# Feature rows on all partitions: by transfers through DRAM on GpSimd's queue in place of TensorE and ScalarE

## What is computed

```python
c_act = jax.nn.silu(c)
for i in range(2):
    mod = c_act @ w_mod[i] + b_mod[i]                      # 6 x 1024 features
    sh1, sc1, g1, sh2, sc2, g2 = jnp.split(mod, 6, axis=-1)
    h = modulate(rmsnorm(x, norm_mix[i]), sh1, sc1)
    y = pool_mixer(h, ...) if i == 0 else moba_attention(h, ...)   # pool_mixer ends in * pool_scale
    x = x + g1[:, None, :] * y
    h = modulate(rmsnorm(x, norm_mlp[i]), sh2, sc2)
    x = x + g2[:, None, :] * squared_relu_mlp(h, w_up[i], w_down[i])
return rmsnorm(x, norm_final)
```

## Time and profile before

| | us |
|---|---|
| median of 3 executions | 1222.71 (1221.52 to 1223.18) |
| the profiled execution | 1221.15 |
| its span, first to last instruction | 1219.4 |
| TensorE busy in it | 1149.8 (94%) |
| VectorE / ScalarE / GpSimd busy | 807.2 / 590.8 / 53.2 |

### The profile page before, as it was taken

How to read it: one execution, slowest core, us unless ns; L and a number is a source line. 1 busy time by engine, 2 the same in 40 slices (tenths; PEclk the granted TensorE clock), 3 DMA queues, 4 the chain that set the end, 5 groups by cost and what they waited for, 6 DMA issues and landing times.

```text
span 1219.4 us, 18071 instructions
## 1 busy us (share of the span) xinstructions
PE 1149.8 (94%) x7384; PEld 1010.6 (83%) x7384; DVE 807.2 (66%) x1287; ACT 590.8 (48%) x914; POOL 53.2 (4%) x103
## 2 busy tenths in 40 slices
PE   5899999999999999999999579999989998999997
PEld 5767659999988776999998479999979887999996
DVE  5558257777776666787777759677783656655554
ACT  6344455444455666644344554434365544543442
POOL 1100000000000001000000000000010000000000
PEclk9999999999999999999999689999999998999999
DMA  8423157977758988798775039877635433555530
GB/s 313 164 74 139 35 211 288 353 269 271 300 143 164 163 129 137 309 356 308 269 271 222 15 136 369 306 272 270 255 131 181 164 114 121 208 199 180 188 124 35
DMA packets 36274, 248.58 MB, mean 204 GB/s; under 512 B 4560, under 2 KB 4704, under 8 KB 7520
## 3 DMA queue, kind: packets, MB, share of 16 engines
q1 hardware_dynamic: 26640, 189.73, 41.5%
q0 software_dynamic: 9552, 57.69, 18.2%
HBM read 242.55 MB, written 4.19 MB: 202 GB/s over the span
## 4 chain that ended last, share of the span: by engine, by line
PE 84%; DVE 10%; ACT 4%; issue 1%; DMA 1%; SPq 0%; DVEq 0%; ACTq 0%
PE bank L1227 71%; PE bank L1409 2%; PE bank L1643 2%; DVE wlo L710 1%; PE bank L1434 1%; PE bank L1626 1%; ACT vo L435 1%; DVE x L730 1%; DVE wlo L821 1%; PE bank L1458 1%; PE bank L1457 1%; PE bank L1456 1%; DVE work L728 1%; PE bank L1305 1%; DVE ul L757 1%
## 5 line engine op out<-in xcount | busy, mean ns | idle before, releaser
L710 DVE TENSOR_TENSOR wlo<-raw,whi 128x2048 fp32r<-128x2048 f32 (+2 forms) x143 | 324.5, 2274 | 103.3 <-ACT whi L425 103.3
L1227 PE MATMUL bank<-uh,whi 128*128 128x256 f32 x1272 | 367.3, 289 | 0.0
L1227 PE MATMUL bank<-uh,wlo 128*128 128x256 f32 x1272 | 359.8, 283 | 0.0
L1227 PE MATMUL bank<-ul,whi 128*128 128x256 f32 x1272 | 359.7, 283 | 0.0
L425 ACT ACTIVATE whi<-raw 128x2048 fp32r<-128x2048 f32 (+2 forms) x143 | 270.4, 1895 | 2.6 <-DMA raw<-in_stream 2.6
L1227 PEld LDWEIGHTS bank<-uh,whi 128*128 128x128 f32 x1272 | 243.5, 191 | 8.4 <-issue 5.9
L1227 PEld LDWEIGHTS bank<-ul,whi 128*128 128x128 f32 x1272 | 243.6, 192 | 4.0 <-issue 1.9
L1227 PEld LDWEIGHTS bank<-uh,wlo 128*128 128x128 f32 x1272 | 243.5, 191 | 0.0
L1227 PE MATMUL bank<-whi,hh 128*128 128x512 f32 x544 | 214.0, 393 | 0.0
L1227 PE MATMUL bank<-wlo,hh 128*128 128x512 f32 x544 | 212.4, 390 | 0.0
L1227 PE MATMUL bank<-whi,hl 128*128 128x512 f32 x544 | 211.8, 389 | 0.0
(11 more groups left out here) (212 smaller groups left out, 1188.8 us busy)
## 6 DMA issues: line engine op xcount, KB each, us to landing
raw<-in_stream SPq DMA_DIRECT2D x176, 1024.0 KB, 4.9
qk<-in_w_mod POOLq DMA_DIRECT2D x48, 1024.0 KB, 5.6
bias_rows<-gb POOLq DMA_DIRECT2D x16, 192.0 KB, 9.3
u<-bias_rows POOLq DMA_DIRECT2D x16, 128.0 KB, 2.4
raw<-in_stream SPq DMA_DIRECT2D x2, 696.0 KB, 10.3
x<-in_x SPq DMA_DIRECT2D x2, 512.0 KB, 4.8
vo<-in_fin_g POOLq DMA_DIRECT2D x2, 512.0 KB, 6.7
out_y<-vo SPq DMA_DIRECT2D x2, 512.0 KB, 2.6
```

What stands on the lines that cost most here:

```text
L710: nc.vector.tensor_tensor(wlo[:, c % RING, 0:w], raw[:, raw_index(c) % RING, 0:w], whi[:, c % RING, 0:w].bitcast(fp32), ALU.subtract).then ...
L1227: ins = mm(out, st, mv, start=start and i == 0, stop=stop and i == 2, skip_group_check=True)
```

## The change

The five rows no longer come from TensorE and ScalarE. GpSimd writes the 8 columns of 128 floats to a DRAM tensor of 5 rows, in the order of the features (`row_to`: 1024 single floats, each to its own address), and later reads one row of 4 KB to all 128 partitions (`row_from`: 512 KB written), after a wait for the write. VectorE waits for `row_in` where it waited for `spread_out`. The waits of TensorE on `col_ready`, `mod_ready` and `spread_out` go with the products. The diff, context cut:

```diff
+        rdram = nc.dram_tensor("feature_rows", [5, D], fp32, kind="Internal").ap()
@@ GpSimd
+            def row_to(k, col):
+                with nc.allow_non_contiguous_dma(reason="1024 features, once a row"):
+                    pool.dma_start(rdram[k, :].rearrange("(b p) -> p b", p=128), col).then_inc(row_out[k], 16)
+            def row_from(k, dst):
+                pool.wait_ge(row_out[k], 16)
+                pool.dma_start(dst, rdram[k, :].partition_broadcast(128)).then_inc(row_in[k], 16)
...
             pool.dma_start(qk[0:64, KI, :], qk[64:128, KI, :]).then_inc(ki_in, 16)
+            pool.wait_ge(col_ready, 2)
+            row_to(0, cact[:, :])
+            pool.wait_ge(s_max["e"], 8)
+            row_from(0, cb[:, :])
             pool.wait_ge(bias_sb, 1)
             for m in range(3):
...
                 elif m == 1:
+                    pool.wait_ge(mod_ready, 1)
+                    row_to(1, gpool[:, :])
                     for h in range(16):
                         pool.wait_ge(used, DIFF + h)
...
                 if m == 1:
                     pool.dma_start(fing, a["fin_g"].partition_broadcast(128)).then_inc(in_fin, 16)
+                    row_from(1, gateb)
                 for i in range(16):
                     g = 16 * m + i
+                    if m == 2 and i == 2:
+                        pool.wait_ge(mod_ready, 2)
+                        row_to(2, mod[:, 40:48])
+                    elif m == 2 and i == 4:
+                        pool.wait_ge(x_ready, x_no(6, 1, 1))
+                        row_from(2, gateb)
...
+            pool.wait_ge(mod_ready, 3)
+            row_to(3, mod[:, 64:72])
+            row_to(4, mod[:, 88:96])
+            row_from(3, cb[:, :])
             pool.wait_ge(bias_out, 256)
             pool.wait_ge(ul_ready, ul_no(8, 0))
...
             pool.dma_start(fing, a["fin_g2"].partition_broadcast(128)).then_inc(in_fin, 16)
+            row_from(4, gateb)
@@ ScalarE: spread_copy and its five calls
-                nc.scalar.activation(dst[:, 512 * j:512 * j + 512], bank[b0 + j][:, :], ACT.Copy).then_inc(spread_out, 1)
@@ VectorE, five times
-            dve.wait_ge(spread_out, 4)
+            dve.wait_ge(row_in[1], 16)
@@ TensorE: spread_col, its five calls and their waits
-                if l != 1:
-                    pe.wait_ge(spread_out, (2, 0, 6, 10)[l])
...
-            pe.wait_ge(mod_ready, 1)
-            spread_col(gpool, 2)
-            pe.wait_ge(spread_out, 4)
             for t in range(NT):
                 norm(5, t)
```

More of the change, by code:

```diff
@@ L244, in build @@
         st_done = [sem(f"st_done{j}") for j in range(2)]
-        col_ready, spread, spread_out = sem("col_ready"), sem("spread"), sem("spread_out")
+        col_ready = sem("col_ready")
+        row_out, row_in = [sem(f"row_out{k}") for k in range(5)], [sem(f"row_in{k}") for k in range(5)]
         mod_ready = sem("mod_ready")
@@ L467, in mlp @@
                     nc.scalar.activation(work[:, 2 + t, :], work[:, t, :], ACT.Square).then_inc(tm_sq, 1)
-                    if t == 0 and l != 1:
-                        spread_copy((0, 1, 2, 4)[l], cb if l == 0 else gateb, 6)
                 hi_upto(m0 + 4)
@@ L498, in pair_upper @@
                     .then_inc(oh_ready, 1)
-            def spread_copy(k, dst, b0):
-                act.wait_ge(spread, k + 1)
-                for j in range(2):
-                    nc.scalar.activation(dst[:, 512 * j:512 * j + 512], bank[b0 + j][:, :], ACT.Copy).then_inc(spread_out, 1)
             act.wait_ge(col_ready, 1)
@@ L649, in _ @@
                 deviation(5, (t,))
-            spread_copy(1, gateb, 2)
             act.wait_ge(mod_ready, 1)
@@ L673, in _ @@
                     value_copy(i // 8, 1, 2, MOBA + i - 1, b_v)
-                    if i == 2:
-                        spread_copy(3, cb, 6)
                 if q == 0 and 1 <= i <= 12 and MIXER[i - 1][0] == "f":
@@ L782, in mlp @@
                 if l == 0:
-                    dve.wait_ge(spread_out, 2)
+                    dve.wait_ge(row_in[0], 16)
                 for s in range(2, 16):
@@ L1182, in _ @@
             mlp(2)
-            dve.wait_ge(spread_out, 6)
+            dve.wait_ge(row_in[2], 16)
             add_and_norm(7, gateb)
@@ L1206, in _ @@
                 lo_beside(MOBA, i, q)
-            dve.wait_ge(spread_out, 8)
+            dve.wait_ge(row_in[3], 16)
             add_and_norm(8, cb)
@@ L1210, in _ @@
             mlp(3)
-            dve.wait_ge(spread_out, 10)
+            dve.wait_ge(row_in[4], 16)
             dve.wait_ge(in_fin, 32)
@@ L1307, in norm @@
                         ins.then_inc(turned, 1)
[L1309 to L1314, removed]
             def mlp(l, turns):
@@ L1369, in mlp @@
                 first(0, 1)
-                if l == 0:
-                    pe.wait_ge(col_ready, 2)
-                    spread_col(cact, 6)
-                elif l == 2:
-                    pe.wait_ge(mod_ready, 2)
-                    spread_col(mod[:, 40:48], 6)
-                elif l == 3:
-                    pe.wait_ge(mod_ready, 3)
-                    spread_col(mod[:, 88:96], 6)
                 first(1, 1)
                 up(2)
-                if l != 1:
-                    pe.wait_ge(spread_out, (2, 0, 6, 10)[l])
                 down(0)
@@ L1755, in _ @@
                     both_halves(MOBA, 7)
-                    pe.wait_ge(mod_ready, 3)
-                    spread_col(mod[:, 64:72], 6)
                 elif kind == "v" and j == 1:
```

## The result

| | before | after |
|---|---|---|
| median, us | 1222.95 (1221.52 to 1225.14) | 1232.83 (1232.17 to 1233.32) |
| ratio to before, 95% interval | | 1.0074 [1.0058, 1.0090] |
| profiled execution / its span | 1221.15 / 1219.4 | 1233.32 / 1231.5 |
| granted clock of TensorE, mean | 0.983 | 0.974 |

The account below looks back on a forecast made before the run. TensorE, busy 94% of the span, was taken to bound the kernel. Gains 5.34 + 2.69 + 1.90 = 9.93 us, no stall added, took the median from 1222.71 to 1212.8 us, range 1211.5 to 1218.

Parts of the forecast that it names:

- Rows 0, 2 and 4: Inside mlp(0), mlp(2) and mlp(3): removing TensorE's row products gains 1.78 us each, 5.34 us in all.
- Row 1: Before pooling, at event 5: ScalarE starts its gained copies earlier without the row copies, a gain of 1.90 us.
- Row 3: Start of MoBA: TensorE goes from the last value product to the features without the row, a gain of 2.69 us.
- Rival 4: Row products only filled TensorE waits, so most of the gain isn't there: 1220.2 us or part of it; chance 0.05.
- Step (b): Bias rows in differential attention, held by row 1's wait for mod_ready: cost zero, up to 6 us for the range.
- Rival 2: Stream falls behind beside bias rows, or mlp(1)'s first w_mod blocks land late: stall 1 to 6 us; chance 0.10.
- Step (a): MoBA start: hanks go behind row 3's write, wait and read, yet arrive in time, 1.3 us remaining; no stall.
- L: Landing time of row 3's column write at the MoBA start, taken as 6 us.
- R: Landing of row 3's broadcast, behind which the hanks queue at the MoBA start: 6.7 us median, 9.5 at worst.
- the limit of 14.0: MoBA start: value in us of column-write landing plus broadcast landing at which late hanks begin to stall TensorE.
- rivals 1 to 3: Rival 1: late MoBA hanks, stall 2.0 to 4.8 us, 0.22. Rival 2: late stream, 0.10. Rival 3: slower, 1225.9 us, 0.05.
- slower: Rival 3: MoBA hanks with write plus broadcast landing above 26.3 us; at worst 13.1 us stall, 1225.9 us; chance 0.05.

Follow-up runs that it names:

- e4: Changed kernel with hanks 0 to 7 ahead of column writes 3 and 4, and row 1's write behind the bias rows: 1215.68 us, ratio 0.9932 to before.
- e8: Kernel before with only rows 0, 2 and 4 through memory, row 4's write behind hank 7; rows 1 and 3 as before: 1220.43 us against 1223.63.
- e5: Changed kernel with the column write as 128 runs of 32 B, output in another feature order: 1226.08 us, ratio 1.0021 to before.
- e9: Changed kernel with bias rows paced two chunks later and hanks 0 to 7 first, row 1's write left in place: 1214.96 us, ratio 0.9937 to before.
- e12: Repeat on another chip: changed kernel with hanks 0 to 7 first and row 1's write behind the bias rows: 1214.86 us against 1223.29 before.
- e1: Kernel before with only a wait for mod_ready added on GpSimd's queue ahead of the sixteen bias rows, no row moved: 1237.98 us against 1225.47.
- e6: Changed kernel with bias rows paced, row h waiting for two more chunks than before: 1224.23 us, ratio 1.0009 to before.
- e7: Kernel before with the wait for mod_ready ahead of the fourth bias row, not the first: 1225.35 us, ratio 1.0011 to before.

## Why the prediction was wrong

**The gains were right, nearly to the number.** Rows 0, 2 and 4: forecast 3 x 1.78 = 5.34, measured 1.8, 1.1 and 1.7 to 1.8, sum 4.7 (e4, e8). Row 1: forecast 1.90, measured 222.2 - 220.3 = 1.9. Row 3: forecast 2.69, measured 2.6 (e4, e5, e9, e12). Sum 9.2 of 9.93. Less the 1.5 us of DIFF it is 7.7, near the 8 us of e4 and e12. Rival 4 falls. The figure of row 4 is the weakest, for the clock is in it: the kernel before had 0.59 and 0.56 from 1024 to 1032, e4 0.69 and then 1.00 from 1020 to 1028. Luck with the clock may have helped there. In the profile of the changed kernel itself two show less: mlp(2) gives 0.6, and mlp(3) 0.1, where the granted clock from 1032 to 1048 was 0.79, 0.50, 0.86 and 0.57.

**Step (b) failed: "I take zero, with up to 6 us for the range".** I had the late start of the bias rows, and that three go out together, but looked at them as a later start of the same train of writes ("for this chunk it starts later and so helps"). The earlier trace rows already held a warning: 8.7 us for a row alone and 17.6 at worst say that rows stand behind one another. Three at once make that queue deeper by one or two just where the stream has 1.2 us to spare. The queue also doesn't stay "full to the end of the layer", in either kernel: before, the rows issued from 372 to 402 took 15.6 to 17.6 us and those from 421 on at most 9.3. The harm is done in the first seven rows. Measured: stream loads of 19.0 us in the median and 20.3 at most became 28.6 and 34.5, ScalarE waited 11.7 us, DIFF +8.1, of which 1.5 are those of e8. e1 shows that the wait alone does it, e6 that it is the rows on their way at once and not the delay. Rival 2 had the mechanism, with 1 to 6 us and a chance of 0.10; both too small.

**Step (a) failed: L was taken as 6, "between" the small moves.** Measured 13.3 to the landing, 13.55 until GpSimd went on, 14.1 with the issue of the read to the hanks. The hank's own landing was 7.3 at the first against R = 6.7. With the prediction's formula L + R = 13.55 + 7.3 = 20.9 against the limit of 14.0 gives a stall of 6.9, and TensorE stood 6.87: the mechanism and the limit were right (that they meet so closely is luck), the term L was mis-sized, 13.55 for 6. The small moves carry 64 runs of 1 KB and 256 runs of 256 B; what counted was the number of runs more than the bytes (e5), and none in the trace had 1024. The rule of the Trainium skill that I quoted against the change (DMA: Bandwidth & Descriptors, Rules for kernel authors: a strided last dimension is one descriptor per element) deserved weight in the choice of L. The runs agree with its direction: 9.0 us against 1.7 with the engines quiet. The same page's 2.0 us plus bytes (Anatomy of one DMA) fits the 128 runs with the engines quiet (1.7); it fails for the 1024 (9.0), and beside other loads for both (4.8 to 10.2 for the 128).

**The clock was not in the sum.** TensorE's long stall was followed by stretches near 1.2 GHz in both places (0.84, 0.50, 0.81 of full speed at MoBA from 936 to 948, 0.63 and 0.51 in DIFF from 412 to 420). It added some 1.7 us at MoBA (8.6 lost for 6.87 idle) and a part in DIFF that I didn't separate. As no run changes the clock alone, its share is argued from the rows and not shown by a run. I had priced stalls at their idle time alone in rivals 1 to 3.

**The rivals together.** Rivals 1 and 2 came true at once. I gave them 0.22 and 0.10 and let each end in the range; neither reached its measured size (8.6 and 8.1), and "slower" was tied to hanks beyond 26.3 us alone. Two losses of separate places add, and that case had no chance of its own.

## What to carry to other kernels

When a transfer is put into a queue ahead of paced transfers, look at what its wait bunches: if the pace of issue is near the time that each takes, a queue once formed drains slowly (here it took the first seven of sixteen rows and a stall), and meanwhile the loads of another queue land late; keep the pace when the start is moved. Price a small transfer by its runs and not by its bytes, and put a write-then-read through memory behind whatever is wanted sooner on that queue. Work taken off the busiest engine brought nearly what its pitch in the timeline said; what decided the sign was the order in the queue that took it over.

## What was not expected of the hardware

- 4 KB as 1024 single floats land after 8.3 to 9.0 us with the DMA engines nearly idle and 11.1 to 17.5 beside other loads, over all kernels here; as 128 runs of 32 B (e5) after 1.7, and 4.8 to 10.2. By the quiet pair, 9.0 and 1.7, 896 more runs cost 7.3 us. On ScalarE's queue 1024 floats took 9.4 and 11.1.
- A write of 192 KB from one partition takes 8.7 us alone; several on their way stand behind one another and land 4 to 8 us apart. With three or four of them unlanded (changed kernel), 1 MB loads on another queue take 28.6 us in the median and 34.5 at most; with two (kernel before) 19.0 and 20.3; with one or two (e6) 14.1 and 16.4. Which resource they share wasn't tested.
- The same idle of TensorE at the same place of the program (2.9 of 4 us) was followed by the full clock in two kernels (before, e7) and by 0.57 of it in e8, 1.5 us apart in DIFF.
